# Experts' down products: the output-bank loop outside the row-group loop

## The chip, the cores and the metric

The kernel runs on one core of a Trainium2 chip. The metric is the device time of one execution in microseconds, as the median of three runs. Engines are named as in the profile: PE is TensorE's matmuls, PEld its weight loads (each matmul instruction has one, which puts the stationary operand into the array), DVE is VectorE, ACT is ScalarE, POOL is GpSimd and SP is SyncE, which issues most of the DMAs.

## What is computed

A decoder trunk of two layers over 256 tokens of width 1024, in float32: a recurrent mixer with a dense SwiGLU, then windowed attention with a mixture of eight SwiGLU experts of which each token takes two. The change is in the experts' last product:

```python
def swiglu(h, w_gate, w_up, w_down):
    return (jax.nn.silu(h @ w_gate) * (h @ w_up)) @ w_down
...
    for e in range(N_EXPERTS):
        out = out + comb[..., e:e + 1].astype(h.dtype) * swiglu(h, w_gate[e], w_up[e], w_down[e])
```

Here D_MODEL is 1024 and D_FF, the inner width, is 3584.

## The kernel before

**Pieces.** The weights of the experts are streamed from HBM in pieces of 1 MB (128 partitions x 2048 floats). The inner width is cut into NCH = 14 chunks of 256. A chunk has three pieces: gate and up (eight row groups of 128 by 256 columns) and down (two row groups of 128, index `f`, by 1024 output columns). SP loads each piece into one of 14 slots of `ring` once the piece that lay there has been split.

**Splitting.** A float32 product is made of three passes in float32r, over high and low parts: `PASSES = ((0, 0), (1, 0), (0, 1))`, where the first index picks the high or low part of the activations and the second that of the weights. ACT makes the high part of each weight piece (L674, `w_hi`, signalled by `hi_done`), and DVE the low part, the difference (L1267, `w_lo`, signalled by `lo_done`). Both have three buffers. ACT may overwrite a buffer when PE has counted the piece as used (`parts_used`, raised by the last matmul of a piece).

**An expert on PE.** Up to 96 tokens (CAP) are gathered for an expert. For a chunk `c`, `gate_up` (L1887) makes 48 matmuls: gate and up, three passes, eight row groups. The stationary operand is the tokens' `xg_hi` or `xg_lo` (128 x 96), the moving one 256 columns of the weights. All 24 of one piece add into the same half bank of PSUM. ACT and DVE then make the hidden values `h_tok`; `turn_h` (L1894) turns them with two transposes, and ACT and DVE store them as `ht_hi` and `ht_lo` (`ht_ready`). Two chunks later `down` (L1909) multiplies them by the down piece: three passes, two row groups `f`, two banks `g` of 512 output columns, 12 matmuls of 512 columns. The stationary operand is `hs[a][:, c % 2, f]`, the same for both `g`. They add into banks 2 and 3 over all 14 chunks of an expert; after the last of them, ACT copies both banks (`keep_y`, L703), and for the last expert ACT and DVE copy one each (L695, L1288).

The order on PE is written out by hand: `gate_up(c)`, `down(c - 2)`, `turn_h(c - 1)`. In chunk 11 the rows of the next expert are turned as well (`turn_rows`, L1876, eight transposes), and in chunks 10 and 11 of the last expert rows of `h` (`turn_back`, L1946). Between experts, `cross` interleaves the last two chunks' downs with the next expert's first two gate and up products. After the last chunk `finish` makes the last two downs and the weighted scatter (L1954). Eight experts of 14 chunks make 112 calls of `down`.

Two products elsewhere are looked at for comparison: the dense layer's down (L1614; 256 columns moving, weights stationary), whose consecutive matmuls add into the same place two by two, and the attention's qkv projection (L1653), where each matmul adds into another place than the one before it.

Of the kernel before, what the change touches and what calls it, by code (L numbers as in the profile page):

```python
# [119 lines left out]
def trunk(nc, x, positions, params, lru_gates, lru_w_in, lru_w_out, attn_w_qkv, attn_b_qkv, attn_sinks, attn_w_o,  # L120
          ffn_w_gate, ffn_w_up, ffn_w_down, moe_w_gate, moe_w_up, moe_w_down, norm_final, consts, out):
    with ExitStack() as ctx:
# [1359 lines left out]
        def _(pe):  # L1482
# [368 lines left out]
            def parts(i, n):  # L1851

                pe.wait_ge(hi_done, PIECES * i + (SPLITS + n + 1))
                return w_hi[:, (SPLITS + n) % PARTS], w_lo[:, (SPLITS + n) % PARTS]

            def low_part(i, n):

                pe.wait_ge(lo_done, PIECES * i + (SPLITS + n + 1))
# [39 lines left out]
            def down(i, c, n, first=False):  # L1898
                w = [a.rearrange("p (f d) -> p f d", f=2) for a in parts(i, n)]
                pe.wait_ge(ht_ready, NCH * i + (c + 1))  # L1900
                if c == 0 and not first:
                    pe.wait_ge(y_staged, 2 * i)
                hs = (ht_hi, ht_lo)
                for a, b in PASSES:
                    if b:
                        low_part(i, n)
                    for f in range(2):
                        for g in range(2):
                            mm = nc.tensor.matmul(ps[0:CAP, 2 + g, :], hs[a][:, c % 2, f], w[b][:, f, g * 512:(g + 1) * 512],  # L1909
                                                  start=(c == 0 and f == 0 and (a, b) == (0, 0)),  # L1910
                                                  stop=(c == NCH - 1 and f == 1 and b == 1))
                mm.then_inc(parts_used, 1)
# [7 lines left out]
            def body(i, to_come, first=False, final=False):  # L1920
                for c in range(2, NCH):
                    n = BODY_AT + 3 * (c - 2)
                    gate_up(i, c, n)
                    down(i, c - 2, n + 2, first)
                    if c == 11 and to_come:
                        turn_rows(i + 1)
                    if final and c in (10, 11):
                        turn_back(c - 10)
                    turn_h(i, c - 1)

            def cross(i):
                pe.wait_ge(xg_ready, 2 * i + 4)
                gate_up(i, 0, END_AT)
                down(i, NCH - 2, END_AT + 2)
                turn_h(i, NCH - 1)
                gate_up(i, 1, END_AT + 3)
                down(i, NCH - 1, END_AT + 5)
                turn_h(i + 1, 0)
# [99 lines left out]
```

## Time and profile before

| what | value |
|---|---|
| median of three runs | 1427.83 us (1426.93 to 1427.84) |
| the profiled execution: its time | 1427.31 us |
| the profiled execution: its span, first to last instruction | 1425.4 us |
| PE busy in the span | 1394.6 us, 98% |
| PEld busy in the span | 1271.4 us, 89% |
| DVE and ACT busy in the span | 80% and 65% |
| granted TensorE clock, mean | 0.991 |

The span is 1.9 us shorter than the execution's time; what is left lies ahead of the first and behind the last instruction. PE's busy time counts an instruction from its start to its modelled end. Matmuls overlap one another, so the time that one takes of the engine is the distance from its start to the start of the next, not its duration.

### The profile page before, as it was taken

To read this page: it belongs to the slowest core of one execution; us is meant where nothing else is said; L and a number is where in the kernel's file an instruction comes from. 1 tells how busy PE (TensorE), PEld (TensorE's weight loads), DVE (VectorE), ACT (ScalarE), POOL (GpSimd) and SP (SyncE) were. 2 spreads that over 40 slices of the span, in tenths; PEclk is the share of its full clock that TensorE was granted. 3 is DMA by queue.
4 is the path that set the end of the run, shared out by engine and by line. 5 is a ranking of instruction groups with operands and counts; after the bars stand their busy time and mean duration, and the time that the engine had idled before them with its cause. 6 is when DMAs were issued, how large, how long until landed. Compare 5 with 4: busy or idle time off the path is not lost.

```text
span 1425.4 us, 24795 instructions
## 1 busy us (share of the span) xinstructions
PE 1394.6 (98%) x10390; PEld 1271.4 (89%) x10390; DVE 1141.3 (80%) x1043; ACT 922.9 (65%) x904; POOL 61.1 (4%) x72
## 2 busy tenths in 40 slices
PE   7999999999999999999999999999999999999995
PEld 6899999998889998889988899988998889998893
DVE  6686565568655998888988888888888888888985
ACT  3745444344535777777777777777777777777764
POOL 2030000003011200000000000000000000000030
PEclk9999999999998999999999999999999999999998
DMA  8456765563217999999999999999999999999941
GB/s 341 144 211 230 249 224 198 187 205 138 102 46 315 403 410 395 380 391 369 368 375 394 357 392 394 357 381 385 383 363 383 395 359 384 385 363 384 373 151 46
DMA packets 63582, 438.64 MB, mean 308 GB/s; under 512 B 7550, under 2 KB 7678, under 8 KB 12272
## 3 DMA queue, kind: packets, MB, share of 16 engines
q1 hardware_dynamic: 58752, 422.60, 77.9%
q10 hardware_dynamic: 3568, 10.57, 2.2%
q0 software_dynamic: 1152, 3.88, 0.8%
q8 instruction: 84, 1.38, 0.4%
q14 instruction: 26, 0.21, 0.0%
HBM read 431.44 MB, written 9.04 MB: 309 GB/s over the span
## 4 chain that ended last, share of the span: by engine, by line
PE 96%; DVE 1%; POOL 1%; ACT 1%; issue 1%; DMA 0%; DVEq 0%; ACTq 0%; SPq 0%; POOLq 0%
PE ps L1887 43%; PE ps L1909 22%; PE ps L1591 11%; PE ps L1614 5%; PE ps L1505 3%; PE ps L1653 2%; PE ps L1537 2%; PE ps L1756 1%; PE ps L1894 1%; PE ps L1700 1%; PE ps L1520 1%; POOL hn L1441 1%; PE ps L1728 1%; PE ps L1866 0%; DMA ring<-in_lru_w_in 0%
## 5 line engine op out<-in xcount | busy, mean ns | idle before, releaser
L1267 DVE TENSOR_TENSOR w_lo<-ring,w_hi 128x2048 fp32r<-128x2048 f32 x336 | 767.4, 2291 | 102.1 <-ACT w_hi L674 101.3
L674 ACT CAST w_hi<-ring 128x2048 fp32r<-128x2048 f32 x336 | 641.0, 1911 | 148.4 <-PE ps L1887 148.3
L1887 PE MATMUL ps<-w_hi,xg_hi 128*96 128x256 f32 x1792 | 248.3, 281 | 1.2 <-DVE xg_lo L1273 1.2
L1887 PE MATMUL ps<-w_hi,xg_lo 128*96 128x256 f32 x1792 | 240.5, 277 | 0.0
L1887 PE MATMUL ps<-w_lo,xg_hi 128*96 128x256 f32 x1792 | 240.5, 276 | 0.0
L1887 PEld LDWEIGHTS ps<-w_hi,xg_lo 128*96 128x96 f32 x1792 | 214.7, 161 | 0.0
L1887 PEld LDWEIGHTS ps<-w_lo,xg_hi 128*96 128x96 f32 x1792 | 214.6, 161 | 0.0
L1887 PEld LDWEIGHTS ps<-w_hi,xg_hi 128*96 128x96 f32 x1792 | 212.8, 161 | 1.3 <-DVE xg_lo L1273 1.3
L864 DVE TENSOR_TENSOR w_lo<-ring,w_hi 128x2048 fp32r<-128x2048 f32 x56 | 130.1, 2325 | 73.8 <-ACT w_hi L487 73.7
L487 ACT CAST w_hi<-ring 128x2048 fp32r<-128x2048 f32 x56 | 106.7, 1907 | 98.3 <-PE ps L1591 87.4
L1909 PE MATMUL ps<-w_lo,ht_hi 128*96 128x512 f32 x448 | 124.8, 400 | 0.0
L1909 PE MATMUL ps<-w_hi,ht_hi 128*96 128x512 f32 x448 | 122.6, 395 | 2.0 <-ACT w_hi L674 2.0
L1909 PE MATMUL ps<-w_hi,ht_lo 128*96 128x512 f32 x448 | 122.3, 395 | 0.0
L1909 PEld LDWEIGHTS ps<-w_lo,ht_hi 128*96 128x96 f32 x448 | 72.5, 162 | 33.3 <-DVE w_lo L1267 0.5
L1909 PEld LDWEIGHTS ps<-w_hi,ht_lo 128*96 128x96 f32 x448 | 72.4, 162 | 31.6
L691 ACT CAST ht_hi<-ps 128x192 fp32r<-128x192 f32 x112 | 35.8, 319 | 77.8 <-PE ps L1894 77.7
L1909 PEld LDWEIGHTS ps<-w_hi,ht_hi 128*96 128x96 f32 x448 | 67.3, 162 | 17.7 <-ACT w_hi L674 2.2
L1591 PE MATMUL ps<-u_hi,w_hi 128*128 128x256 f32 x448 | 55.8, 277 | 0.0
L1591 PE MATMUL ps<-u_hi,w_lo 128*128 128x256 f32 x448 | 55.5, 276 | 0.0
L1591 PE MATMUL ps<-u_lo,w_hi 128*128 128x256 f32 x448 | 55.5, 276 | 0.0
L1591 PEld LDWEIGHTS ps<-u_hi,w_hi 128*128 128x128 f32 x448 | 53.0, 188 | 0.5 <-issue 0.4
L1591 PEld LDWEIGHTS ps<-u_lo,w_hi 128*128 128x128 f32 x448 | 52.9, 188 | 0.0
(285 smaller groups left out, 1243.5 us busy)
## 6 DMA issues: line engine op xcount, KB each, us to landing
ring<-in_moe_w_gate SPq DMA_DIRECT2D x112, 1024.0 KB, 7.2
ring<-in_moe_w_up SPq DMA_DIRECT2D x112, 1024.0 KB, 7.1
ring<-in_moe_w_down SPq DMA_DIRECT2D x112, 1024.0 KB, 7.3
ring<-in_ffn_w_gate SPq DMA_DIRECT2D x14, 1024.0 KB, 4.9
ring<-in_ffn_w_up SPq DMA_DIRECT2D x14, 1024.0 KB, 5.1
ring<-in_ffn_w_down SPq DMA_DIRECT2D x14, 1024.0 KB, 4.9
ring<-in_lru_w_in SPq DMA_DIRECT2D x7, 1024.0 KB, 12.4
ring<-in_attn_w_qkv SPq DMA_DIRECT2D x6, 1024.0 KB, 4.8
```

Of the source, the lines that this page charges most:

```text
L487: nc.scalar.copy(w_hi[:, j % PARTS], ring[:, slot_at(j)]).then_inc(hi_done, 1)
L674: nc.scalar.copy(w_hi[:, (SPLITS + n) % PARTS], ring[:, s]).then_inc(hi_done, 1)
L691: nc.scalar.copy(ht_hi[:, c % 2], ps[:, 6 + c % 2, 0:2 * CAP].rearrange("p (f n) -> p f n", f=2)).then_inc(ht_hi_ready, 1)
L864: V.tensor_tensor(w_lo[:, j % PARTS], ring[:, slot_at(j)], w_hi[:, j % PARTS].bitcast(F32), ALU.subtract).then_inc(lo_done, 1)
L1267: V.tensor_tensor(w_lo[:, part], ring[:, ORDER_MOE[n % SLOTS]], w_hi[:, part].bitcast(F32), ALU.subtract).then_inc(lo_done, 1)
L1505: mm = nc.tensor.matmul(ps[:, p % 4, f * T:(f + 1) * T], col[:, k, f * P:(f + 1) * P], u_raw[:, k], start=(k == 0), stop=(k == KC - 1))
L1537: mm = nc.tensor.matmul(ps[:, p, f * T:(f + 1) * T], w[b][:, k, f * P:(f + 1) * P], zs[a][:, k], start=False, stop=(k == KC - 1 and b == 1 ...
L1591: mm = nc.tensor.matmul(ps[:, 2 * (c % 2) + f, m * T:(m + 1) * T], w[b][:, k, f * P:(f + 1) * P], us[a][:, k], start=(j > 1 and k == 0 and ...
L1614: mm = nc.tensor.matmul(ps[:, 4 + d // 2, (d % 2) * T:(d % 2 + 1) * T], w[b][:, f, d * P:(d + 1) * P], fs[a][:, c % 2, f], start=False, st ...
L1653: mm = nc.tensor.matmul(ps[:, a % 2, b * T:(b + 1) * T], us[m][:, k, b * P:(b + 1) * P], w[n][:, k], start=False, stop=(k == KC - 1 and m ...
L1887: mm = nc.tensor.matmul(ps[0:CAP, c % 2, m * CHF:(m + 1) * CHF], xs[a][:, k], w[b][:, k], start=(k == 0 and (a, b) == (0, 0)), stop=(k == ...
L1909: mm = nc.tensor.matmul(ps[0:CAP, 2 + g, :], hs[a][:, c % 2, f], w[b][:, f, g * 512:(g + 1) * 512], start=(c == 0 and f == 0 and (a, b) == ...
```

## The change

In `down` the two inner loops change places. The 12 matmuls of a piece, their operands and their number are the same. Within a pass the order was (f0, bank 2), (f0, bank 3), (f1, bank 2), (f1, bank 3), and becomes (f0, bank 2), (f1, bank 2), (f0, bank 3), (f1, bank 3).

```diff
                 for a, b in PASSES:
                     if b:
                         low_part(i, n)
-                    for f in range(2):
-                        for g in range(2):
+                    for g in range(2):
+                        for f in range(2):
                             mm = nc.tensor.matmul(ps[0:CAP, 2 + g, :], hs[a][:, c % 2, f], w[b][:, f, g * 512:(g + 1) * 512],
                                                   start=(c == 0 and f == 0 and (a, b) == (0, 0)),
                                                   stop=(c == NCH - 1 and f == 1 and b == 1))
```

## Rows read from the trace of the kernel before

**Rows 1.** The page: busy time, share and instructions of each engine.

```profile
PE 1394.6 (98%) x10390; PEld 1271.4 (89%) x10390; DVE 1141.3 (80%) x1043; ACT 922.9 (65%) x904; POOL 61.1 (4%) x72
```

**Rows 2.** Stretches: the experts' first pieces, and all up to the last downs.

```profile
core 0: us, PE busy (x) PEld busy (x) DVE busy (x) ACT busy (x) POOL busy (x), PEclk, DMA share, GB/s
...
450.00:467.00 17.00, 15.84 (x141) 15.83 (x141) 14.17 (x14) 16.89 (x15) 0.00 (x0) 1.00 1.01 421
467.00:1399.00 932.00, 931.29 (x6855) 833.87 (x6853) 831.32 (x612) 690.58 (x577) 18.68 (x10) 1.00 0.96 369
```

**Rows 3.** The waits of PE between 467 and 1412 us, all of them.

```profile
PE ps L1909 <- ACT w_hi L674: 2.0, 1, 2.0
PE ps L1954 <- issue: 0.9, 1, 0.9
```

**Rows 4.** The waits of ACT and DVE between 467 and 1399 us, the longest.

```profile
ACT w_hi L674 <- PE ps L1887: 148.3, 202, 0.9
DVE w_lo L1267 <- ACT w_hi L674: 97.0, 261, 1.3
...
ACT hn L703 <- PE ps L1909: 5.8, 7, 0.8
```

**Rows 5.** The chain that ended last, 900 to 940 us (start, us, what).

```profile
904.11 5.44 PE ps L1887 x48
909.55 2.80 PE ps L1909 x12
912.35 0.17 PE ps L1894 x2
912.52 5.61 PE ps L1887 x48
...
926.70 2.80 PE ps L1909 x12
...
929.67 5.45 PE ps L1887 x48
```

**Rows 6.** PE in order of time around the down of chunk 10, fourth expert (start, us).

```profile
908.48 1.07 PE L1887 MATMUL ps<-w_lo,xg_hi 128*96 128x256 f32 x8
909.39 1.09 PE L1909 MATMUL ps<-w_hi,ht_hi 128*96 128x512 f32 x4
910.32 1.08 PE L1909 MATMUL ps<-w_hi,ht_lo 128*96 128x512 f32 x4
911.24 1.11 PE L1909 MATMUL ps<-w_lo,ht_hi 128*96 128x512 f32 x4
912.19 0.33 PE L1894 MATMUL ps<-cst,hn 96*128 96x96 f32 x2
```

**Rows 7.** One line's instructions (L1909): duration in ns, min/median/max.

```profile
L1909 PEld LDWEIGHTS ps<-w_hi,ht_hi x448: 159/162/283, 467.7 to 1405.5; 128*96 128x96 f32 x150
L1909 PE MATMUL ps<-w_hi,ht_hi x448: 388/395/672, 467.8 to 1405.7; 128*96 128x512 f32 x150
```

**Rows 8.** PE in order of time, dense down, then the qkv projection twice.

```profile
252.52 1.98 PE L1614 MATMUL ps<-f_hi,w_hi 128*128 128x256 f32 x16
254.34 1.86 PE L1614 MATMUL ps<-f_lo,w_hi 128*128 128x256 f32 x15
...
346.63 1.98 PE L1653 MATMUL ps<-w_lo,u_hi 128*128 128x256 f32 x16
348.44 1.98 PE L1653 MATMUL ps<-w_hi,u_lo 128*128 128x256 f32 x16
...
364.30 2.05 PE L1653 MATMUL ps<-w_lo,u_hi 128*128 128x256 f32 x16
366.19 2.05 PE L1653 MATMUL ps<-w_hi,u_lo 128*128 128x256 f32 x16
```

**Rows 9.** The chain at the last expert's end.

```profile
1400.34 4.34 PE ps L1909 x12
...
1405.11 2.90 PE ps L1909 x12
```

## What the change does to the time: the prediction

> **What bounds the kernel now.** I read the page's engine list first: PE is busy for 98% of the span, far ahead of DVE at 80% and ACT at 65% [rows 1]. The two stretches of the experts then show whether that holds there. From 467 to 1399 us, which is 932 of the 1425.4 us, PE is busy for 931.29 us at a granted clock of 1.00, the 2.4 GHz level [rows 2]. DMA is busy for 0.96 of this stretch, which could be a bound of its own, so the waits come next: up to the last expert's end PE waits once for ACT's high part (2.0 us, in the last but one down) and once before the scatter (0.9 us), and never for a DMA [rows 3]. It is the others that wait for PE: ACT 148.3 us before its high parts, and DVE in turn 97.0 us for ACT [rows 4]. The reader is to see one thing: whatever changes the pace of PE's matmuls in this stretch changes the time one to one, and what only eases the others changes nothing.
>
> The chain that ended last gives the terms. It runs through PE alone: 48 matmuls of gate and up in 5.44 us, 12 of down in 2.80 us, two transposes in 0.17 us, again and again [rows 5]. All 112 downs stand in it, some 112 x 2.80 = 314 us.
>
> **The change part by part.**
>
> *Counts.* Nothing is added or removed. Each of a pass's four matmuls has its own weight load before the change, also where the stationary operand is the one that already lies in the array: 448 loads stand beside 448 matmuls for each pass [rows 7]. After it there are again 12 loads, 12 matmuls and one count of `parts_used` per down. No wait moves: the first instruction of a piece waits for the high part and for `ht_ready`, the first of the third pass for the low part, and the last raises `parts_used`. So SP, ACT, DVE and POOL are told the same things at the same places. Term: 0 us.
>
> *Weight loads.* The order before repeats the stationary operand in two of four matmuls, the new order changes it at each. If repeated loads were cheaper, this would cost. The rows say that a load is hidden anyway: it takes 162 ns [rows 7], less than the 230 ns or so between two matmuls of down, and gate and up, where each load brings other data, run a matmul every 5.44 / 48 = 113 ns [rows 5], shorter than one load's own duration. Term: 0 us. Cover gone, at most 6 more new loads x 162 ns x 112 = 109 us would come on top; that end is excluded by the gate and up rows and isn't used for the range. The Trainium skill (TensorE: Matmul & The Clock Gate, Step-by-step: what each phase is for) speaks against the change: it has weights loaded once and used for many matmuls. By that rule the order before would be the better one; this trace shows 448 loads of 448, so nothing here is reused.
>
> *Banks.* The new order adds twice into bank 2, then twice into bank 3, instead of in turn. No row isolates this for 512 columns. Of the near rows, the dense down adds two by two into the same place and goes at (254.34 - 252.52) / 16 = 114 ns for 256 columns; the qkv projection changes place at each matmul and goes at (366.19 - 364.30) / 16 = 118 ns, but once, in the same code, at (348.44 - 346.63) / 16 = 113 ns [rows 8]. So 113 and 117 or so are two paces at which one and the same code runs, and the place of the output doesn't choose between them. Gate and up show the same pair: 5.44 and 5.61 us for 48 [rows 5]; the longer form stands 17 times in the chain, twice in each of seven experts and three times in the last, always after the eight extra transposes.
>
> *The pace of the downs.* In the down of [rows 6] the passes take 910.32 - 909.39 = 0.93, 911.24 - 910.32 = 0.92 and 912.19 - 911.24 = 0.95 us, 230 to 238 ns for a matmul. At gate and up's fast pace per column 12 matmuls of 512 columns would take 5.44 / 2 = 2.72 us; they take 2.80. That 0.08 us is the only thing in a down that an order of matmuls could give back: 112 x 0.08 = 9.0 us, the lower end. The upper end is all three passes at the slowest one's 0.95: 2.85 us, 112 x 0.05 = 5.6 us more. Which value? A down takes 2.80 us after gate and up of 5.44 and also, at 926.70, after one of 5.62 [rows 5]. The 12 matmuls keep their sum whichever pace PE came in with, so I take 2.80 us after the change too. Term: 0 us. (The Trainium skill's section Back-to-back issue gap, on the same page, gives columns / 2.4 + 2.5, 216 ns for 512 columns, whatever bank they go to; it knows no order either. By it a down would be 2.59 us, before and after; the rows show 2.80, and by both the change is worth 0.)
>
> *Evacuation.* Bank 2 is now complete two matmuls before the end, but ACT's copies wait for `parts_used`, which the last matmul raises. They stand behind PE for 5.8 us in seven crossings [rows 4], and nothing on PE waits for them. Term: 0 us.
>
> *The end.* The last two downs take 4.34 and 2.90 us [rows 9], the first because the granted clock falls to its lower level, 1.2 GHz, during it, after PE's wait of 2.0 us [rows 3]. Were that fall to miss the down, 4.34 - 2.80 = 1.5 us would be saved; I take it as it is.
>
> Sum: 0 us on a profiled execution of 1427.31 us (span 1425.4 and 1.9 around it), which is 0.5 us below the median of 1427.83. Forecast: 1427.8 us.
>
> **The rivals.**
>
> *The downs take up the fast pace.* If adding to one bank twice in a row is what lets 512 columns run as gate and up do, up to 9.0 us go: 1418.8 us. For it: the downs' 2.80 us is above 2.72, the dense down, in pairs, runs at the fast pace [rows 8], and gate and up, which never change their place within a piece, do so mostly. Against it: the qkv projection, with one and the same alternation, runs at both [rows 8]. It decides by more than 0.2% from 2.9 / 112 = 26 ns per down, a third of the gap. Chance 0.24.
>
> *The downs go slower throughout.* The new order could hold all passes at the pace of the third: 112 x 0.05 = 5.6 us, 1433.4 us. Against it: nothing says why the third pass is the slow one, but both orders offer it the same operands. Chance 0.11.
>
> *The pieces after the downs fall to the lower pace.* This is the one with the largest price: gate and up run at one of two paces, and which one is settled in the first matmuls behind a down and its transposes. If the new order ends a down otherwise, the 95 pieces of 5.44 us could take 5.61: 95 x (5.61 - 5.44) = 16.2 us, 1444.0 us. It decides from 2.9 / 0.17 = 17 pieces on, which would be two more for each expert. For it: eight transposes more ahead of them suffice to cause it [rows 5]. Against it: it happened in 17 of 112 places only. Chance 0.10. The reverse, all 17 pieces of 5.61 us back at 5.44, gives 17 x 0.17 = 2.9 us, 1424.9 us, the edge of what can be told; chance 0.04 of passing it, with some gain in the downs.
>
> *A repeated load is cheaper than the rows let it look.* Then the time is above 1431; chance 0.03, for the reasons given.
>
> *DMA as the bound of a faster PE.* With 9.0 us less in 932 the experts' 369 GB/s would become 373; DMA moved 421 while it filled the ring [rows 2]. It would not take the gain away.
>
> **How the numbers follow.** Forecast 0.48; faster downs 0.24 and faster pieces 0.04; slower downs 0.11, slow pieces 0.10, loads 0.03. 0.2%, or 2.9 us, is about what a measurement of this kernel can tell from no change. Faster 0.28, same 0.48, slower 0.24. The likeliest case's own range is 1425.0 to 1430.7. The range has to take in both bounds of the downs' pace, 1418.8 and 1433.4, which I round outwards to 1418.5 and 1434.0; what is left out is the slow pieces in larger number and the dear loads, about 0.12.
>
> **What would show it.** In the profile of the changed kernel: 448 weight loads per pass at about 162 ns; 12 matmuls of down in 2.80 us in the chain, whatever stands ahead; 48 of gate and up in 5.44 us, and in 5.61 at the same 17 places; PE busy for 931 us of the same stretch, and no wait but that of 2.0 us and that before the scatter. A down of 2.72 us would make the first rival right, 2.85 the second; more or fewer gate and up pieces of 5.6 us the third. Single matmuls of a down further apart where the row group changes than elsewhere would point to the loads. A granted clock that falls at another place near 1400 us would shift the end by up to 1.5 us without any of these.

## The result: slower by 0.56%, and how the profile shows it

The changed kernel takes 1435.97 us (median of 6 runs, 1433.63 to 1437.71); the kernel before took 1427.84 us beside it (6 runs, 1426.93 to 1429.15). The ratio is 1.0056 with a 95% interval of 1.0044 to 1.0068. The profiled execution has a span of 1434.0 us, 8.6 us more than before. The forecast was no change, with a range up to 1434.0, and the median lies 2.0 us above it.

PE's instructions are the same in number. The page's engine list of the changed kernel answers to [rows 1], the stretch of the experts to [rows 2]:

```profile
PE 1402.9 (98%) x10390; PEld 1284.1 (90%) x10390; DVE 1141.3 (80%) x1043; ACT 922.5 (64%) x904; POOL 61.3 (4%) x72
```

```profile
467.00:1399.00 932.00, 932.00 (x6791) 839.63 (x6790) 823.08 (x605) 686.81 (x572) 18.79 (x10) 1.00 0.96 368
```

PE is busy without a gap at the same clock, but the same 932 us hold 6791 matmuls where they held 6855. DMA moves 368 GB/s for 369. The waits of PE from 467 to 1420 us say the same, all of them (line, releaser: us, times, longest), beside [rows 3]:

```profile
PE ps L1909 <- ACT w_hi L674: 2.0, 1, 2.0
PE ps L1954 <- issue: 0.9, 1, 0.9
PE ps L1909 <- DVE w_lo L1267: 0.2, 1, 0.2
```

So no new wait of any size: PE's own matmuls stand further apart. The chain that ended last shows which (start, us, what), beside [rows 5]:

```profile
562.34 2.76 PE ps L1909 x12
565.10 0.17 PE ps L1894 x2
565.27 5.61 PE ps L1887 x48
570.87 2.76 PE ps L1909 x12
573.63 0.17 PE ps L1894 x2
573.80 5.62 PE ps L1887 x48
```

The downs are shorter, 2.76 us for 2.80. The untouched 48 matmuls of gate and up take 5.61 or 5.62 us each time, where 5.44 to 5.46 was the rule. Of the 110 pieces that stand alone in the chain, 93 took about 5.46 us and 17 about 5.62 before; after the change it is 6 and 104.

The account, from the experts' first matmul to the end of the last transposes, which is 9.8 us longer (451.17 to 1398.14 us before, 451.12 to 1407.91 after): the chain's gate and up sum to 614.2 us before and 628.1 after, 14.0 more. Of that, 87 more long pieces at 0.158 us each (0.16 below) make 13.7, and 0.3 is in the first piece, two products in one, which goes from 11.14 to 11.45 us. The 110 downs up to there sum to 307.8 and 303.6 us, 4.2 less. The end gives some back. Chain, beside [rows 9]:

```profile
1408.15 1.91 ACT w_hi L674
1410.08 2.30 DVE w_lo L1267
1412.43 1.17 PE ps L1909 x4
...
1413.82 2.78 PE ps L1909 x12
```

The granted clock stays at 1.00 in the last two downs this time, and from the end of the last transposes to the end of the last down it takes 8.7 us (1407.91 to 1416.60), where it took 9.9 (1398.14 to 1408.01). That is 1.2 us less, and 14.0 - 4.2 - 1.2 = 8.6 us is the whole difference of the spans.

Within a down, in order of time (start, us), beside [rows 6]:

```profile
562.18 1.08 PE L1909 MATMUL ps<-w_hi,ht_hi 128*96 128x512 f32 x4
563.09 1.08 PE L1909 MATMUL ps<-w_hi,ht_lo 128*96 128x512 f32 x4
564.01 1.09 PE L1909 MATMUL ps<-w_lo,ht_hi 128*96 128x512 f32 x4
564.94 0.33 PE L1894 MATMUL ps<-cst,hn 96*128 96x96 f32 x2
```

The passes take 0.91, 0.92 and 0.93 us, where they took 0.93, 0.92 and 0.95. The weight loads of the changed line are as many and as long as those of [rows 7]:

```profile
L1909 PEld LDWEIGHTS ps<-w_hi,ht_hi x448: 159/161/163, 467.9 to 1414.1; 128*96 128x96 f32 x150
L1909 PE MATMUL ps<-w_hi,ht_hi x448: 388/392/478, 468.0 to 1414.4; 128*96 128x512 f32 x150
```

Two questions are left: what makes the downs shorter, and what makes the pieces after them longer. Below, a piece is "short" at 5.46 us or so and "long" at 5.62; the counts are of the 110 pieces that stand alone in each kernel's chain. The single starts in the trace say where a pace is settled: before and after the change the first three distances between starts are alike in short and long pieces (on average 174 or 175, 118 to 120, 118 or 119 ns); from the fourth on they differ, and soon stand at 113, 113, 114 or 117, 117, 116 ns in turn. That is 113.3 and 116.7 ns, which at 2.4 GHz (granted clock 1.00) works out to 272 and 280 cycles.

### The profile page after: what moved, and what is told of

The parts are those of the page before. It is cut to its first block, busy times and chain, and to the rows that moved or that the text cites. A ratio compares the mean times of both kernels' runs of the same rounds, so it can differ in the third digit from the quotient of the medians.

```text
span 1434.0 us, 24795 instructions
## 1 busy us (share of the span) xinstructions
PE 1402.9 (98%) x10390; PEld 1284.1 (90%) x10390; DVE 1141.3 (80%) x1043; ACT 922.5 (64%) x904; POOL 61.3 (4%) x72
## 4 chain that ended last, share of the span: by engine, by line
PE 96%; DVE 1%; POOL 1%; ACT 1%; issue 1%; DMA 0%; DVEq 0%; ACTq 0%; POOLq 0%
PE ps L1887 44%; PE ps L1909 21%; PE ps L1591 11%; PE ps L1614 5%; PE ps L1505 3%; PE ps L1653 2%; PE ps L1537 2%; PE ps L1756 1%; PE ps L1894 1%; PE ps L1700 1%; PE ps L1520 1%; POOL hn L1441 1%; PE ps L1728 0%; PE ps L1866 0%; POOL hn L1444 0%
## 5 line engine op out<-in xcount | busy, mean ns | idle before, releaser
L1887 PE MATMUL ps<-w_hi,xg_hi 128*96 128x256 f32 x1792 | 252.5, 283 | 1.2 <-DVE xg_lo L1273 1.2
L1887 PE MATMUL ps<-w_hi,xg_lo 128*96 128x256 f32 x1792 | 245.4, 279 | 0.0
L1887 PE MATMUL ps<-w_lo,xg_hi 128*96 128x256 f32 x1792 | 245.1, 278 | 0.0
L1887 PEld LDWEIGHTS ps<-w_hi,xg_lo 128*96 128x96 f32 x1792 | 219.5, 162 | 0.0
L1887 PEld LDWEIGHTS ps<-w_lo,xg_hi 128*96 128x96 f32 x1792 | 218.9, 161 | 0.0
L1887 PEld LDWEIGHTS ps<-w_hi,xg_hi 128*96 128x96 f32 x1792 | 216.1, 162 | 1.3 <-DVE xg_lo L1273 1.3
L1909 PE MATMUL ps<-w_hi,ht_hi 128*96 128x512 f32 x448 | 120.9, 392 | 2.0 <-ACT w_hi L674 2.0
L1909 PE MATMUL ps<-w_lo,ht_hi 128*96 128x512 f32 x448 | 122.2, 394 | 0.2 <-DVE w_lo L1267 0.2
L1909 PE MATMUL ps<-w_hi,ht_lo 128*96 128x512 f32 x448 | 121.0, 391 | 0.0
L1909 PEld LDWEIGHTS ps<-w_lo,ht_hi 128*96 128x96 f32 x448 | 72.3, 161 | 31.7 <-DVE w_lo L1267 0.7
L1909 PEld LDWEIGHTS ps<-w_hi,ht_lo 128*96 128x96 f32 x448 | 72.0, 161 | 30.6
L1909 PEld LDWEIGHTS ps<-w_hi,ht_hi 128*96 128x96 f32 x448 | 67.2, 161 | 17.6 <-ACT w_hi L674 2.2
L1591 PEld LDWEIGHTS ps<-u_hi,w_lo 128*128 128x128 f32 x448 | 52.9, 188 | 0.0
```

What stands on the lines that cost most here:

```text
L1591: mm = nc.tensor.matmul(ps[:, 2 * (c % 2) + f, m * T:(m + 1) * T], w[b][:, k, f * P:(f + 1) * P], us[a][:, k], start=(j > 1 and k == 0 and ...
L1887: mm = nc.tensor.matmul(ps[0:CAP, c % 2, m * CHF:(m + 1) * CHF], xs[a][:, k], w[b][:, k], start=(k == 0 and (a, b) == (0, 0)), stop=(k == ...
```

## The experiments

All times are medians; the kernel before, run beside them, took 1427.1 to 1427.9 us.

**e1 and e2: which pass counts.** e1 puts only the third pass into the new order, e2 only the first two.

```diff
-                    for g in range(2):
-                        for f in range(2):
+                    for f, g in (NEW if b else OLD):    # e1; e2 has the two exchanged
...
```

NEW and OLD stand for the two lists of four pairs.

> Only the third pass of a down (low weights) takes the new order; the first two keep the old one. Theory A (the last matmuls of a down leave gate and up at one of two paces): the third pass alone decides, so most of the 112 gate and up pieces take 5.66 us as in the changed kernel, about 1438 us. Theory B (what the engines beside PE do in the first gate and up matmuls decides, and the down's shorter length of 2.76 us shifts them): the down gets shorter by a third of 0.04 us only, and most pieces stay at 5.44, 5.45 or 5.51 us from the start of the first matmul; about 1427 us.

> The first two passes take the new order, the third keeps the old one. Theory A: gate and up stay at the shorter time (95 or so of 112) and the downs keep part of their gain, 2.77 to 2.79 us; about 1424 to 1426 us. Theory B: a down of about 2.77 us shifts the others nearly as the changed kernel does, most pieces take 5.66 us, about 1437 us.

e1 took 1420.85 us (median of five executions), ratio 0.9950 (0.9934 to 0.9967), but one of them, the profiled one, 1429.03 us. e2 took 1424.39 us in ten, ratio 1.0016 (0.9982 to 1.0049): six between 1422.8 and 1424.6, four between 1437.2 and 1438.7, nothing between; its profiled execution, 1424.62 us, has 102 short and 8 long. Neither theory holds: e1 is far from theory A's 1438 us and mostly below theory B's 1427, and e2 meets A's time in six executions and B's in four. In e1's profile 44 pieces are long and 66 short, in a nearly fixed round (chain, start, us):

```profile
607.78 5.46 PE ps L1887 x48
613.24 2.78 PE ps L1909 x12
616.01 0.17 PE ps L1894 x2
616.18 5.62 PE ps L1887 x48
621.80 2.79 PE ps L1909 x12
624.59 0.17 PE ps L1894 x2
624.76 5.46 PE ps L1887 x48
```

A piece after the same down and the same transposes is short once and long the next time. So the order of a pass doesn't fix the pace; it changes which pace follows on which.

**e3 and e8: the transposes ahead of the down,** in the new order (e3) and in the old (e8).

```diff
                     gate_up(i, c, n)
+                    turn_h(i, c - 1)
                     down(i, c - 2, n + 2, first)
...
-                    turn_h(i, c - 1)
```

> New order, and within an expert's chunks the two transposes stand ahead of the down instead of behind it, so that gate and up follow the down's last matmul at once. Theory C (the pace is drawn anew behind the transposes, with their 96 rows and their short matmuls, and the down only shifts the draw): gate and up are mostly at 113 ns for a matmul, and the 62 ns gap behind the transposes goes to the front of the down; about 1424 us. Theories A and B: gate and up behind a down of the new order still take the longer pace, 1434 to 1437 us.

> Old order, and the two transposes stand ahead of the down. With the new order this took 1423.9 us, with 60 gate and up pieces at the shorter pace. If the gain was the place of the transposes, the old order gains as well and lies at 1420 to 1425 us; if it was the new order's shorter downs with fewer long pieces, the old order stays at 1427 us or above.

e3: 1423.86 us in seven executions, ratio 0.9972 (0.9961 to 0.9984), with 60 short and 50 long pieces. e8: 1425.16 us in ten, ratio 0.9985 (0.9976 to 0.9995), 82 short and 28 long. Both beat the kernel before, though both have more long pieces than its 17. The gain is at the end (e8's chain, beside [rows 9]):

```profile
1399.70 0.17 PE ps L1894 x2
1399.87 2.85 PE ps L1909 x12
...
1402.94 2.79 PE ps L1909 x12
```

ACT stores `ht_hi` ahead of the next high part. In e8 it can do so while PE is still in the down: it starts that high part at 1397.25 us, and PE ends the down at 1399.70. Before, the transposes came behind the down, which ended at 1397.96, and ACT started at 1398.38. So PE's wait of 2.0 us is gone, and the granted clock stays at 1.00. From the end of the last gate and up to the end of the last down it is 9.0 us in e3 and e8, where it was 12.8. So the 2 us of e8 are these 3.8 us less what 11 more long pieces cost, and e3 adds shorter downs and 33 more long pieces to the same. The pieces still change pace without transposes right ahead of them, so theory C in its plain form falls.

**e4: 24 matmuls of 256 columns for 12 of 512.**

```diff
-                    for g in range(2):
+                    for q in range(4):
                         for f in range(2):
-                            mm = nc.tensor.matmul(ps[0:CAP, 2 + g, :], hs[a][:, c % 2, f], w[b][:, f, g * 512:(g + 1) * 512],
+                            mm = nc.tensor.matmul(ps[0:CAP, 2 + q // 2, (q % 2) * 256:(q % 2 + 1) * 256], hs[a][:, c % 2, f],
+                                                  w[b][:, f, q * 256:(q + 1) * 256],
...
```

> Each down matmul of 512 columns is cut into two of 256, in the new order's manner (two row groups into one place, then the next place): 24 matmuls and 24 weight loads for 12. Theory D (matmuls of 512 columns have no pace of their own and wander, which knocks gate and up from one pace to the other; those of 256 keep the pace they enter with): a down takes 24 x 113 = 2.72 us, gate and up 5.44 throughout, 112 x 0.08 + 17 x 0.17 = 12 us less than before, about 1416 us. If 256 columns at the longer pace lock in too: 24 x 117 = 2.81 us and gate and up 5.61, about 1443 us.

1428.48 us in ten executions (one of them, of 3974 us, is not explained by anything here), ratio 0.9999 (0.9989 to 1.0009). Its chain:

```profile
562.61 2.80 PE ps L1909 x24
565.42 0.17 PE ps L1894 x2
565.58 5.46 PE ps L1887 x48
571.04 2.72 PE ps L1909 x24
573.76 0.17 PE ps L1894 x2
573.93 5.62 PE ps L1887 x48
579.55 2.80 PE ps L1909 x24
```

Theory D is right in one half: the 24 keep the pace they enter with, 2.72 us after a short piece and 2.80 after a long one. In the other half it falls: without any 512-column matmul in the downs, pieces still change pace, here mostly at every second, 54 short and 56 long.

**e5: ACT and DVE nearly idle.** Both split 128 of 2048 columns of each expert piece.

```diff
-                V.tensor_tensor(w_lo[:, part], ring[:, ORDER_MOE[n % SLOTS]], w_hi[:, part].bitcast(F32),
+                V.tensor_tensor(w_lo[:, part, 0:128], ring[:, ORDER_MOE[n % SLOTS], 0:128], w_hi[:, part, 0:128].bitcast(F32),
...
-                nc.scalar.copy(w_hi[:, (SPLITS + n) % PARTS], ring[:, s]).then_inc(hi_done, 1)
+                nc.scalar.copy(w_hi[:, (SPLITS + n) % PARTS, 0:128], ring[:, s, 0:128]).then_inc(hi_done, 1)
```

> New order; ACT's high part and DVE's low part of the experts' pieces are computed for 128 of 2048 columns only, the rest of both buffers keeps what lay there, so the experts' products are not the reference's. PE's instructions are the same, ACT and DVE are nearly idle. If the longer pace of gate and up comes from reads or writes of ACT and DVE beside PE, all pieces take 5.51 us from the start of the first matmul and the time falls to about 1420 us. If it is PE's own, left to it by the matmuls before, some 100 of 112 pieces take 5.66 to 5.68 us as before, about 1434 us.

One execution, 1434.05 us. The stretch of the experts (busy us of PE, PEld, DVE, ACT, POOL; clock, DMA) and the chain:

```profile
467.00:1399.00 932.00, 932.00 (x6791) 839.68 (x6790) 182.48 (x596) 163.52 (x570) 11.01 (x10) 1.00 0.96 368
```

```profile
565.71 5.62 PE ps L1887 x48
571.33 2.76 PE ps L1909 x12
574.09 0.17 PE ps L1894 x2
574.26 5.61 PE ps L1887 x48
```

DVE's busy time falls from 823 to 182 us and ACT's from 687 to 164, and PE makes the same 6791 matmuls in the stretch; 107 pieces are long, 3 short. With three quarters of their work gone the longer pace stays, so it doesn't come from ACT and DVE beside PE. (The expectation's 5.51 us counts from the first matmul's start; the chain shows the same piece as 5.46.)

**e6 and e9: stationary operand or banks.** Two more orders of the four matmuls of a pass.

```diff
+                    for f, g in ((0, 0), (0, 1), (1, 1), (1, 0)):    # e6, serpentine
...
+                    for f, g in ((0, 0), (1, 1), (0, 1), (1, 0)):    # e9, diagonal
```

> Order within a pass: (f0, bank 2), (f0, bank 3), (f1, bank 3), (f1, bank 2). The stationary operand repeats as in the old order, and banks change at every second matmul as in the new one. If the banks make the new order's third pass shorter (0.92 for 0.95 us), this has it too, and a down takes about 2.76 us; if it is the change of the stationary operand at every matmul, a down takes 2.80 us as before. How many gate and up pieces take 5.66 us neither theory tells: between 0 and 112, 1419 to 1438 us.

> Order within a pass: (f0, bank 2), (f1, bank 3), (f0, bank 3), (f1, bank 2). The stationary operand changes at every matmul as in the new order; the banks go 2, 3, 3, 2 as in the serpentine order, which left the downs at the old 2.80 us. If the stationary operand's change is what shortens a down, it takes 2.76 us here, and the gate and up pieces behave as in the changed kernel, about 1436 us. If it is the order in which the weights are read (row group outside or inside), a down takes 2.80 us, about 1427 us.

In e6 the downs of the chain average 2.80 us, in e9 2.75. One down of each in order of time, first e6:

```profile
562.49 1.09 PE L1909 MATMUL ps<-w_hi,ht_hi 128*96 128x512 f32 x4
563.42 1.08 PE L1909 MATMUL ps<-w_hi,ht_lo 128*96 128x512 f32 x4
564.34 1.10 PE L1909 MATMUL ps<-w_lo,ht_hi 128*96 128x512 f32 x4
565.28 0.33 PE L1894 MATMUL ps<-cst,hn 96*128 96x96 f32 x2
```

Then e9:

```profile
560.74 1.08 PE L1909 MATMUL ps<-w_hi,ht_hi 128*96 128x512 f32 x4
561.65 1.08 PE L1909 MATMUL ps<-w_hi,ht_lo 128*96 128x512 f32 x4
562.58 1.08 PE L1909 MATMUL ps<-w_lo,ht_hi 128*96 128x512 f32 x4
563.49 0.33 PE L1894 MATMUL ps<-cst,hn 96*128 96x96 f32 x2
```

e6 changes banks as seldom as the new order but keeps the stationary operand for two matmuls, and it has the old passes: 0.93, 0.92, 0.94. e9 has e6's banks but a new stationary operand at every matmul, and its passes are 0.91, 0.93, 0.91. So a down is shorter where the row group `f` changes at every matmul, whatever the banks do. `f` picks the stationary operand and also the row group of the weights that move past it; no run changes one without the other, so that it is the stationary operand, and not the order in which the moving weights are read, is not shown.

The times: e6 1427.85 us in ten executions, ratio 1.0006 (0.9997 to 1.0016), with 87 short and 23 long. e9 1436.84 us in nine, ratio 1.0067 (1.0056 to 1.0077), and here is the clearest sight of all: eight executions took 1436.3 to 1438.1 us, and the profiled one 1420.1, with 108 short pieces and 2 long. 17 us between two executions of one program is about 108 x 0.16: the pieces were nearly all short in the one and, by this arithmetic, nearly all long in the others (their pieces can't be read). In e1 and e9 the profiled execution is the odd one out; in e2 and e13 both groups of times are met among the others too.

**e7 and e12: a third transpose** (the second one made twice), in the new order (e7) and in the old (e12).

```diff
-                for f in range(2):
+                for f in (0, 1, 1):
                     mm = nc.tensor.transpose(ps[:, 6 + c % 2, f * CAP:(f + 1) * CAP], h_tok[:, c % 2, f * P:(f + 1) * P],
```

> New order, and the second of the two transposes of the hidden values is made twice, into the same place: 112 more matmuls of 96 columns between down and gate and up, 30 to 90 ns each, 3 to 10 us if nothing else changes (1439 to 1446 us). If the pace of gate and up hangs on the moment at which they begin behind the short matmuls, a large part of the 105 long pieces changes, each by 0.16 us, and the time may fall below the changed kernel's in spite of the added work. If the down alone decides, the pieces stay at 5.66 us.

> Old order, with the third transpose. It adds 112 x 0.086 = 9.6 us. The old order has 17 long pieces of 112; if the third transpose takes all to the shorter pace, 2.7 us come back and the time is about 1435 us, above the new order with the same addition (1429.9 us) by the 112 x 0.04 us of the downs. If it makes more pieces long, the time is above 1440 us.

e7 took 1429.93 us in eight executions, ratio 1.0020 (1.0010 to 1.0031): 6 us less than the changed kernel (5 us by the two ratios, each to its own runs of the kernel before), with 112 matmuls more. Its chain:

```profile
561.72 2.76 PE ps L1909 x12
564.49 0.25 PE ps L1894 x3
564.73 5.46 PE ps L1887 x48
570.19 2.76 PE ps L1909 x12
572.95 0.25 PE ps L1894 x3
573.20 5.46 PE ps L1887 x48
```

The transposes take 0.25 us for 0.17, 9 us in all, and 107 pieces of 110 are short, which gives 101 x 0.16 = 16 us back. In the old order the same addition does the reverse: e12 took 1439.87 us (two executions), ratio 1.0089 (1.0069 to 1.0110), with 55 pieces short and 55 long, every second one. The expectation had 1435 us for pieces all short, and above 1440 us for more long ones; it is the second case.

**e10, e11, e14, e15: other small matmuls between down and gate and up,** all in the new order, ahead of the transposes (e10, e14) or behind them (e11, e15); of float32 with 96 rows (e10, e11) or bf16 with one row (e14, e15).

```diff
+                nc.tensor.matmul(ps[0:CAP, 6 + c % 2, 256:264], cst[0:CAP, 0:CAP], cst[0:CAP, 0:8], start=True, stop=True)
...
+                nc.tensor.matmul(ps[0:CAP, 6 + c % 2, 256:264], zero[:, 0:CAP], zero[:, 0:8], start=True, stop=True)
```

> New order, and one small matmul (96 rows, 96 x 8) between a down and its two transposes, into columns that nobody reads. If any further matmul in this place takes gate and up back to the shorter pace, as the third transpose did, 105 pieces save 0.16 us each, 17 us, against 112 x 0.03 to 0.09 us of its own: 1422 to 1429 us. If the third transpose worked by its own length or place (86 ns, last before gate and up), the pieces stay at 5.66 us, 1439 to 1446 us.

> The same small matmul behind the two transposes, last before gate and up. If what counts is the matmul that stands right ahead of gate and up, this one differs from e10; otherwise the two are alike: 1422 to 1429 us with the pieces at the shorter pace, 1439 to 1446 us without.

> New order, and ahead of the two transposes a bf16 matmul with one row (1 x 96 by 1 x 8). It is shorter than the third transpose's 86 ns. If a shift of gate and up's start is what frees them from the longer pace, whatever its size, most pieces take 5.51 us and the time is 1420 to 1426 us; if only some shifts do, they stay at 5.66 us and it is 1438 to 1442 us.

> The same matmul behind the two transposes. Same two readings as for e14: 1420 to 1426 us with gate and up at the shorter pace, 1438 to 1442 us at the longer.

| run | us | ratio (95% interval) | short | long |
|---|---|---|---|---|
| e10 | 1441.20 | 1.0097 (1.0080 to 1.0114) | 76 | 34 |
| e11 | 1439.18 | 1.0083 (1.0066 to 1.0099) | 106 | 4 |
| e14 | 1464.06 | 1.0255 (1.0240 to 1.0270) | 39 | 71 |
| e15 | 1455.61 | 1.0200 (1.0185 to 1.0215) | 107, see below | 3 |

In e11 the short pieces read 5.53 us, the long 5.70. In e15 107 read 5.64 us, but their first two matmuls stand 200 ns apart where others stand 175, and the matmuls from the sixth on 113, so they are short ones that begin late; the last three read 5.77 to 5.79. Each insertion gives another pattern, none of them the all-long one of the changed kernel, and each costs more than it brings: the one-row matmul of e14 makes what stands between down and gate and up 0.45 us long for 0.17. My sizes for these were far too low.

**e13 and e16.** e13 is e1 again; e16 is e1 with the transposes ahead of the down.

> The kernel of e1 once more, with more executions: four of its five took 1419.8 to 1421.8 us and one 1429.0 us. If two patterns of paces are open to one and the same program, the executions fall into groups at about 1420.5 and 1429 us and nothing between; if e1's first was a stray, all lie at 1420 to 1422 us.

> Third pass of the down in the new order as in e1, and the transposes ahead of the down as in e3 and e8, which both gained 2 to 4 us. If the gains add, 1417 to 1419 us; if the place of the transposes only changes which pieces run at which pace, the time is one of those seen, 1420 to 1430 us.

e13: 1424.23 us in twelve executions, ratio 0.9984 (0.9969 to 0.9999): six at 1420.3 to 1421.8, six at 1426.7 to 1429.3, so two patterns, as the first reading had it. Its profiled execution took 1421.33 us and has 104 short pieces and 6 long; e1's took 1429.03 with 66 and 44. The 38 pieces x 0.16 = 6.1 us are most of the 7.7 between them; longer downs (2.78 us on average for 2.77) add 0.9. e16: 1435.32 us in four, ratio 1.0058 (1.0043 to 1.0072), 10 short and 100 long. It keeps the gain of e3 and e8 at the end (no wait for the high part, last downs of 2.85 and 2.81 us), and yet two edits that gained alone lose together: 100 long pieces outweigh both gains.

## Why the prediction was wrong

- **What bounds the kernel: right.** PE's pace sets the time from the first expert to the last transposes; it moved the time without a wait, and e5 shows that ACT's and DVE's work doesn't enter there. At the end it does, by the wait of 2.0 us for ACT's high part.
- **Counts, weight loads, evacuation, DMA: right.** The same 448 loads for each pass, 161 ns each; no new wait of PE above 0.2 us; 368 GB/s. The rule of the Trainium skill (TensorE: Matmul & The Clock Gate, Step-by-step: what each phase is for) that weights are loaded once and used for many matmuls did not decide: in both orders every matmul has its own load, and the order that never repeats a stationary operand has the shorter downs, 2.76 us for 2.80.
- **"The place of the output doesn't choose between them":** for the length of the downs the place plays no part, by e6 and e9; for the pace of gate and up it was not tested by itself. The first rival, that adding twice to one bank is what shortens a down, had the effect but not the cause, and half of its size: 0.04 us of 0.08.
- **"The 12 matmuls keep their sum whichever pace PE came in with, so I take 2.80 us after the change too": wrong.** That the sum hardly depends on the pace PE came in with is right here (2.79 to 2.80 us before, 2.76 after; e1 and e2 show 0.01 to 0.03 us), but it says nothing of another order, and the order changed it. Measured: 4.2 us less, 0.04 for each down.
- **The step that failed:** the forecast left the gate and up pieces as they were, "48 of gate and up in 5.44 us, and in 5.61 at the same 17 places". The third rival named exactly what happened, with its price, at a chance of 0.10 and outside the range; "it happened in 17 of 112 places only" was taken as evidence that it was rare. But those places came in a fixed pattern after a fixed disturbance, which suggests that the pace follows from what PE did before, piece after piece. In such a case one edit can flip all of them. 104 long for 17 is 13.7 us, near the rival's 16.2. The runs confirm the size, not how the order sets the pace: that cause stays open.
- **The range** took each rival alone. The shorter downs and the long pieces came together: 1427.8 - 4.2 + 14.0, less 1.2 at the end, = 1436.4, and the median was 1435.97.
- **The end:** named as uncertain by up to 1.5 us, and 1.2 us came back there.

What is shown: the time follows the number of long pieces, the length of the downs and what PE waits for at the end; the longer pace stays when ACT and DVE do a quarter of their work; one program's times fall into two groups from one execution to the next (e1 with e13, e2, e9). What is open: what carries the pace from one piece to the next, and why the new order has nearly all long in its profile, with six executions at 1433.6 to 1437.7 us, while e9, with downs of about the same length, once had nearly all short. Whether the DMAs play a part in the experts was not tried. Outside them the trace of the kernel before has a hint: the qkv projection that [rows 8] shows at 118 ns ran with the DMAs busy for 0.03 of the time (columns as in [rows 2]):

```profile
364.30:368.00 3.70, 3.70 (x34) 3.70 (x33) 0.26 (x2) 3.70 (x12) 0.00 (x0) 1.00 0.03 11
```

So a pace of 118 ns doesn't need busy DMAs there. A run of matmuls without weight loads between them was not tried either.

The best kernel whose executions all lie together is e3's, 1423.86 us, with the new order and the transposes ahead of the down; all its seven executions lie at 1422.5 to 1425.6. e1's kernel has the lower median, 1421.77 us over the seventeen executions of e1 and e13: ten took 1419.8 to 1421.8 us, but seven 1426.7 to 1429.3.

## What to carry to other kernels

Where PE is never idle, read the distance from one matmul's start to the next, group by group, before and after: the same instructions can run at two paces 3% apart, and an edit that shortens one group can move all its neighbours to the other. If a profile shows such a pair of paces, count the pieces at each and price the case that all of them flip, together with every other effect, before calling an edit neutral. Compare many executions of a candidate: a median over two patterns moves with how often each is met.

## What the runs showed of the hardware that I had not expected

- Matmuls of 256 columns in float32r with a 96-column weight load each have two steady distances, 113.3 and 116.7 ns (5.46 and 5.62 us for 48), at a granted clock of 1.00 in both; the two differ from the fourth distance of a piece on and hold to its end, and the longer one stays when ACT and DVE are nearly idle (e5).
- Matmuls of 512 columns take 2.80 us for 12 when the stationary operand repeats in pairs (before, e6) and 2.75 to 2.76 when it, and the row group of the moving weights with it, changes each time (after, e9).
- The time of one program can differ by 17 us in 1420 from one execution to the next at the same mean granted clock, 0.990 and 0.990 to 0.992, and the count of long pieces accounts for it (e9; of the longer executions by arithmetic only).
- Adding 112 transposes, 0.08 us each, made the changed kernel 5 to 6 us shorter (e7).
- A bf16 matmul of one row and 8 columns ahead of the float32 transposes cost 0.28 us each time: the stretch between down and gate and up grew from 0.17 to 0.45 us (e14).
